# One product by ones instead of eight, for the convolution's mean and mean of squares: VectorE adds the chunks first

## The chip, the cores and the metric

The kernel runs on one core of a Trainium2 chip. The metric is the device time of one execution in microseconds (us): the median of the runs of one kernel. Before the change it is 1557.03 us over three runs (1554.2, 1557.03 and 1557.95).

## What is computed

The program is two transformer blocks one behind the other, on 256 tokens of width 1024, all in float32. Only a piece of the first block matters here, the convolution branch, and in it the layer norm behind the depthwise convolution:

```python
def layer_norm(x, g, b):
    xf = x.astype(jnp.float32)
    mu = jnp.mean(xf, axis=-1, keepdims=True)
    var = jnp.mean(jnp.square(xf - mu), axis=-1, keepdims=True)
    y = (xf - mu) * lax.rsqrt(var + EPS) * g.astype(jnp.float32) + b.astype(jnp.float32)
    return y.astype(x.dtype)

def conformer_conv(u, conv_w, conv_b, ln_g, ln_b, w_pw):
    a, g = jnp.split(u, 2, axis=-1)
    y = a * jax.nn.sigmoid(g)
    y = lax.conv_general_dilated(y, conv_w[:, None, :], ...) + conv_b
    y = jax.nn.silu(layer_norm(y, ln_g, ln_b))
    return y @ w_pw
```

Here `y` has 256 tokens by 1024 channels, and the mean and the mean of squares are taken over the channels. The same block computes queries, keys and values for attention, two gates, and behind them attention, a merge of the branches, and a feed-forward part that gathers single neurons from a table. The second block has two kinds of attention and a mixture of experts.

## The kernel before, in words

The kernel is written out by hand for the five engines: each engine has one instruction stream (`block.tensor`, `block.vector`, `block.scalar`, `block.gpsimd`, `block.sync`), and semaphores join them. Nothing reorders an engine's stream: an instruction that waits holds up all that stands behind it on its engine.

Activations lie with channels on the 128 partitions and tokens along a row, so 1024 channels are K = 8 chunks of 128 x 256. A sum over channels is thus a sum over partitions and chunks. TensorE makes it: `stat` (L643) multiplies by a 128 x 128 matrix of ones and accumulates the chunks in a bank of PSUM, one product a chunk. A float32 product is two MATMUL instructions in the profile, so the eight products of a stat are 16.

The stretch around the change is the projection of the first block, from about 60 to 230 us of the span:

- TensorE follows `first_order()` (L181): pieces `glu` and `gate` of the input projection in split products (L711 and L716), between them the parts of a modulation (`modulation`, L674) and sums of these. Near its end, ahead of the last modulation part (`("part", 7)`), stands `("mean", 0)` (L752): it waits until all eight chunks of the convolution are there (`conv_ready`) and makes the stat "mean". After it come the last modulation part, its sums, and then, once the blocks `w_uq` and `w_ukv` of weights have landed (`use`, L774), eight rounds m = 0 to 7 of the products `q`, `k` and `v` (L776 to L785). After round 1 stands the stat "var" (L787), the mean of squares, which waits for ScalarE's squares (`sq_ready`).
- VectorE makes the depthwise convolution (L1782 to L1799), a chunk m at a time: L1786 gates the chunk, L1789 to L1798 add up 31 taps, L1798 writes chunk m of `convz`. Between chunks it does small jobs for the norms of q and kv (L1800 to L1814). Then it reads the mean (L1818), subtracts it from all chunks (L1820), and takes the `q` tiles out of PSUM as they come, four instructions a round (L1827 to L1832). After round 1 it reads the mean of squares (`inverse("var", D)`, L1752 and L1754), after round 3 it scales the chunks (L1837).
- ScalarE rounds weight pieces for the split products, takes tiles out of PSUM, and squares the centred convolution into `sq` (L1380).
- GpSimd subtracts rounded weights from weights (L1700), one piece of 128 x 1024 after the other, and after the last piece of this stretch spreads a rotated key over the heads in two copies (L1697).
- SyncE loads the weight blocks, all through L543, into a ring of three slots. A load waits until the block three places ahead of it has been used; TensorE tells that with `w_used`, on the first product of the block behind. So the load of `w_ukv` is let go by the first product of the last modulation part, the one behind the stat "mean".

`convz` and `sq` lie in the tile `arena`; `hT`, the normed input of the block, is half of the tile `xh` and is not read any more after GpSimd's first eight subtractions (`h_split`, 63.6 to 69.1 us).

Of the kernel before, what the change touches and what calls it, by code (L numbers as in the profile page):

```python
# [24 lines left out]
ALU = mybir.AluOpType  # L25
# [7 lines left out]
K = D // P  # L33
# [240 lines left out]
def build(nc, w, out):  # L274
# [3 lines left out]
    with ExitStack() as ctx:  # L278
# [29 lines left out]
        hT = xh[:, 1]  # L308
# [174 lines left out]
        gain_ready = sem("gain_ready")  # L483
        ctx_norm_ready = sem("ctx_norm_ready")
        h_ready, h_part, sq_part = sem("h_ready"), sem("h_part"), sem("sq_part")
        in_conv = sem("in_conv")
        qkv_norm_ready = sem("qkv_norm_ready")
        krope_ready, kr_spread = sem("krope_ready"), sem("kr_spread")
# [130 lines left out]
        def _(pe):  # L619
# [124 lines left out]
            for kind, n in first_order():  # L744
                if kind == "part":
                    modulation(4 + n, first_block(2 * n + 1), 1)
                elif kind == "u":
                    pair(TILE[f"u{n}"], use(STREAM["w_in"]), 2 * n, hT, 1 - n)
                elif kind == "mod2_":
                    modulation_sums(TILE[f"mod2_{n}"], 4 + 2 * n)  # L750
                elif kind == "mean":
                    pe.wait_ge(conv_ready, K)  # L752
                    stat("mean", ones, chunks(convz))
                elif kind == "ctx":
                    pe.wait_ge(ctx_norm_ready, 1)
                    pair(TILE["ctx0"], use(STREAM["w_in"]), 2, hcT)
                else:
                    i = FIRST.index((kind, n - n % 2))
                    if i == 0:
                        pair(TILE[f"{kind}{n}"], use(first_block(0)), 2 * n, hT, 1 - n, None if n else (h_ready, 0))  # L760
                    else:
                        ps = tile(TILE[f"{kind}{n}"])
                        for j in range(2):
                            c = 4 * (i - 1) + 2 * (n % 2) + j
                            last = split(ps[:, j * T:(j + 1) * T], c, c + 1, h1_hi, h1_lo, (1 - n % 2) * (1 - j),
                                         None if c else (h_split, 0))
                        last.then_inc(tile_ready, 1)
                if (kind, n) == ("glu", 3):
                    pe.wait_ge(sq_ready, 3)
                    stat("q", ones, chunks(sq[:, 0:2, :]))  # L770
                    pe.wait_ge(sq_ready, 4)
                    stat("kv", ones, [sq[:, 2:4, :].rearrange("p a t -> p (a t)")], 2 * T)
# [3 lines left out]
            for m in range(8):  # L776
                ps = tile(TILE[f"q{m}"])
                group(ps[:, 0:T], proj(uq, 2 * m, cqn, 2048, 2), 1 if m == 0 else 0)
                group(ps[:, T:2 * T], proj(uq, 2 * m + 1, cqn, 2048, 2)).then_inc(tile_ready, 1)

                ps = tile(TILE[f"k{m}"])
                group(ps[:, :], [(ukv[:, m * P:(m + 1) * P], ckvn)]).then_inc(tile_ready, 1)
                ps = tile(TILE[f"v{m}"])
                group(ps[:, :], [(ckvn[:, (m // 2) * P:(m // 2 + 1) * P],
                                  ukv[:, D + (m % 2) * 512:D + (m % 2 + 1) * 512])]).then_inc(tile_ready, 1)  # L785
                if m == 1:
                    pe.wait_ge(sq_ready, 5)  # L787
                    stat("var", ones, chunks(sq))

            pe.wait_ge(kr_spread, 2)  # L790
            for kind, n in order:
# [925 lines left out]
        def _(dve):  # L1717
# [64 lines left out]
            for m in range(K):  # L1782

                dve.wait_ge(tile_free["act"], readers[:TILE[f"glu{m}"] + 1].count("act"))
                y = ypad[:, m % 2, :]
                tt(y[:, HALF:HALF + T], cglu[:, m % 4, 0:T], cglu[:, m % 4, T:2 * T], ALU.mult).then_inc(glu_used, 1)  # L1786
                dve.wait_ge(glu_used, m + 1)
                s = [0, 0]
                s[0] = mark(ts(cacc[:, 0, :], y[:, 0:T], conv_w[:, m * TAPS:m * TAPS + 1], vcol("conv_b", m),  # L1789
                               ALU.mult, ALU.add))  # L1790
                s[1] = mark(ts(cacc[:, 1, :], y[:, 1:1 + T], conv_w[:, m * TAPS + 1:m * TAPS + 2], None, ALU.mult))
                for j in range(2, TAPS):
                    dve.wait_ge(dve_step, s[j % 2])
                    acc = cacc[:, j % 2, :]
                    s[j % 2] = mark(stt(cpart if j == TAPS - 2 else acc, y[:, j:j + T],  # L1795
                                        conv_w[:, m * TAPS + j:m * TAPS + j + 1], acc, ALU.mult, ALU.add))
                dve.wait_ge(dve_step, max(s))
                tt(convz[:, m, :], cacc[:, 0, :], cpart, ALU.add).then_inc(conv_ready, 1)  # L1798
                dve.wait_ge(conv_ready, m + 1)  # L1799
                if m == 2:  # L1800

                    dve.wait_ge(tile_free["act"], readers[:TILE["ctx0"] + 1].count("act"))
                    mark(tt(rt1[64:96, 0, 0:T], krope[64:96, 0:T], rope_tab[64:96, :], ALU.mult))
                    seq(tt(rt1[64:96, 0, T:2 * T], krope[96:128, 0:T], rope_tab[96:128, :], ALU.mult))
                    tt(krope[64:96, 0:T], rt1[64:96, 0, 0:T], rt1[64:96, 0, T:2 * T], ALU.add).then_inc(krope_ready, 1)
                    inverse("q", Q_RANK)
                if m == 3:
                    inverse("kv", KV_RANK, 2 * T)
                if m == 5:
                    r = rstd(3)  # L1810
                    for i in range(2):
                        stt(cqn[:, i, :], cq[:, i, :], vcol("q_g", i), r, ALU.mult, ALU.mult).then_inc(qkv_norm_ready, 1)
                    r = rstd(4, 2 * T)
                    stt(ckvn, ckv, vcol("kv_g"), r, ALU.mult, ALU.mult).then_inc(qkv_norm_ready, 1)  # L1814
# [9 lines left out]
            for m in range(8):  # L1824
                ps = take(TILE[f"q{m}"]).rearrange("p (a t) -> p a t", a=2)
                v1, v2 = (x[64:96, m % 2, :].rearrange("p (a t) -> p a t", a=2) for x in (rt1, rt2))
                nc.vector.tensor_copy(qT[0:64, 2 * m:2 * m + 2, :], ps[0:64])  # L1827
                mark(tt(v1, ps[64:96], tab[64], ALU.mult))
                tt(v2, ps[96:128], tab[96], ALU.mult).then_inc(tile_free["dve"], 1)
                dve.wait_ge(dve_step, step[0])  # L1830
                dve.wait_ge(tile_free["dve"], m + 1)
                tt(qT[64:96, 2 * m:2 * m + 2, :], v1, v2, ALU.add).then_inc(q_ready, 1)  # L1832
                if m == 1:
                    inverse("var", D)
                if m == 3:
                    dve.wait_ge(convc_ready, 1)
                    tt(convz, convz, over(rstd(5), K), ALU.mult).then_inc(convn_ready, 1)  # L1837
# [698 lines left out]
```

## Time and profile before

| | |
|---|---|
| median of three runs | 1557.03 us (1554.2 to 1557.95) |
| the profiled execution's own time | 1562.65 us |
| its span, first to last instruction | 1560.8 us |
| TensorE products, busy | 1305.5 us (84% of the span), 7412 instructions |
| VectorE, busy | 868.6 us (56%), 2078 instructions |
| ScalarE, busy | 536.0 us (34%) |
| GpSimd, busy | 438.4 us (28%) |
| mean granted TensorE clock | 0.874 |
| chain of waits that ended last, by engine | TensorE 56%, DMA 30%, VectorE 8%, ScalarE 4% |

The busy shares are means over stages with different limits; what a change in one stage is worth is read from that stage. The chain of waits follows the work back from the last instruction, at each step to what released it. A timeline lists instructions in order of time: start, length, engine, line, operation, output and inputs with their shapes, and in brackets the idle time ahead of it and what ended that. PE is TensorE, PEld its weight loads, DVE VectorE, ACT ScalarE, POOL GpSimd, SP SyncE. The profiled execution took 5.6 us more than the median of the runs.

### The profile page before, as it was taken

Reading aid. Unit: us, or ns where it says so; the run is one execution under the profiler, and the core shown is the slowest. Engines: PE = TensorE matmul, PEld = TensorE weight load, DVE = VectorE, ACT = ScalarE, POOL = GpSimd, SP = SyncE. Lnnn points to the kernel's source line nnn. Section 1 sums busy time; section 2 is a strip of 40 time slices with the busy share of each in tenths; the row PEclk is TensorE's granted clock in tenths of the full one; section 3 lists DMA queues with packets and bytes.
Section 4 is the critical chain, followed back from the end, with each engine's and each line's share of the span. In section 5 each row is a group of like instructions: output and inputs, shape, how many; then the busy total and the mean of one; then the engine's idle time right before and its main releaser. Section 6 shows DMA issues by size and latency. Waiting matters only on the chain.

```text
span 1560.8 us, 19427 instructions
## 1 busy us (share of the span) xinstructions
PE 1305.5 (84%) x7412; PEld 737.8 (47%) x7412; DVE 868.6 (56%) x2078; ACT 536.0 (34%) x1062; POOL 438.4 (28%) x357
## 2 busy tenths in 40 slices
PE   6999999999798666566667766679999999999997
PEld 4888866697443111111111111118769987454544
DVE  2689685654689889854454444544546533321213
ACT  2244264532334333322322222224685501212112
POOL 0555600061334333333333333310535400000000
PEclk9999999999999676766766666769999999999999
DMA  9466612153999999999999999994223356899994
GB/s 388 169 260 239 235 59 102 48 189 108 401 384 397 422 420 421 421 421 421 421 421 421 422 421 421 422 391 197 108 108 109 109 210 278 322 427 427 428 427 203
DMA packets 53086, 476.00 MB, mean 305 GB/s; under 512 B 6145, under 2 KB 6785, under 8 KB 7553
## 3 DMA queue, kind: packets, MB, share of 16 engines
q0 software_dynamic: 36864, 268.45, 41.6%
q1 hardware_dynamic: 14832, 203.46, 32.5%
q10 hardware_dynamic: 1296, 2.84, 0.5%
q8 instruction: 59, 0.97, 0.2%
q14 instruction: 35, 0.28, 0.0%
HBM read 473.68 MB, written 1.05 MB: 304 GB/s over the span
## 4 chain that ended last, share of the span: by engine, by line
PE 56%; DMA 30%; DVE 8%; ACT 4%; issue 2%; POOL 0%; SPq 0%; DVEq 0%; ACTq 0%
DMA arena<-in_uv,pick 25%; PE psD L638 16%; PE psD L711 7%; PE psD L1142 6%; PE psY L888 6%; PE psD L716 4%; PE psD L845 3%; PE psD L1151 3%; DVE arena L1955 3%; ACT arena L1265 2%; DMA arena<-in_experts 2%; PE psY L819 2%; DMA ring<-in_w_in 2%; PE psY L638 1%; ACT L1265 1%
## 5 line engine op out<-in xcount | busy, mean ns | idle before, releaser
L888 PE MATMUL psY<-arena 64*64 64x512 f32 x2048 | 399.0, 873 | 204.8 <-ACT arena L1265 204.4
L1688 POOL DMA_INDIRECT arena<-in_uv,pick x256 | 239.9, 937 | 432.2 <-PE psY L888 385.3
L888 PEld LDWEIGHTS psY<-arena 64*64 64x64 f32 x2048 | 69.4, 169 | 518.8 <-ACT arena L1265 503.4
L1955 DVE CUSTOM_DVE_ANT_0 arena<-arena,psD 128x1024 f32<-128x1024 f32 x128 | 156.2, 1221 | 162.7 <-DMA arena<-in_uv,pick 162.7
L1265 ACT ACTIVATE arena<-arena,pick 128x64 f32<-128x64 f32 x256 | 88.7, 347 | 387.3 <-DVE pick L1955 358.8
L1265 ACT ACTIVATE arena<-psD 64x512 f32<-64x512 f32 (+4 forms) x128 | 68.2, 538 | 330.0 <-PE psD L1142 105.0
L1955 DVE CUSTOM_DVE_ANT_0 arena<-arena,psY 128x1024 f32<-128x1024 f32 x128 | 153.9, 1214 | 44.2 <-DMA arena<-in_uv,pick 43.5
L1265 ACT ACTIVATE arena<-arena 128x64 f32<-128x64 f32 (+2 forms) x300 | 116.0, 387 | 17.2 <-DVE arena L2312 3.8
L638 PE MATMUL psD<-arena 128*128 128x256 f32 (+4 forms) x352 | 92.2, 404 | 0.7 <-DVE arena L2076 0.7
L1795 DVE SCALAR_TENSOR_TENSOR psY<-arena,pick,psY 128x256 f32<-128x256 f32 x224 | 89.2, 482 | 0.0
L638 PE MATMUL psD<-arena,ring 128*128 128x256 f32 (+1 forms) x304 | 73.9, 401 | 4.1 <-issue 3.6
L1265 ACT ACT_TABLE_LOAD x58 | 74.4, 1283 | 7.2 <-DVE pick L1955 4.5
L638 PEld LDWEIGHTS psD<-arena 128*128 128x128 f32 (+2 forms) x352 | 61.4, 193 | 18.1 <-issue 8.1
L638 PEld LDWEIGHTS psD<-arena,ring 128*128 128x128 f32 x304 | 58.8, 195 | 15.8 <-issue 7.0
L845 PE MATMUL psD<-xh,ring 128*128 128x256 f32 x256 | 63.4, 394 | 2.2 <-DVE xh L1920 1.5
L2384 DVE TENSOR_TENSOR yrow_lo<-psD,yrow_hi 64x512 fp32r<-64x512 f32 x32 | 22.0, 689 | 71.4 <-ACT yrow_hi L1265 70.9
L1700 POOL TENSOR_TENSOR ring_r<-ring,work_r 128x1024 fp32r<-128x1024 f32 x9 | 22.8, 2547 | 133.5 <-ACT work_r L1265 133.5
L845 PEld LDWEIGHTS psD<-xh,ring 128*128 128x128 f32 x256 | 47.2, 194 | 23.7 <-issue 15.2
L1265 ACT ACTIVATE arena<-psY 128x512 f32<-128x512 f32 (+1 forms) x50 | 29.7, 594 | 55.5 <-PE psY L804 35.9
L2377 DVE SCALAR_TENSOR_TENSOR arena<-psD,arena 64x512 f32<-64x512 f32 x16 | 12.1, 756 | 47.8 <-ACT arena L1265 47.6
L1265 ACT ACTIVATE arena<-xh 128x512 f32<-128x512 f32 (+1 forms) x17 | 11.9, 704 | 76.3 <-DVE xh L2249 57.2
L1142 PE MATMUL psD<-arena,xh 128*64 128x512 f32 x160 | 36.5, 594 | 1.1 <-DMA arena<-in_experts 1.1
(373 smaller groups left out, 2316.9 us busy)
## 6 DMA issues: line engine op xcount, KB each, us to landing
arena<-in_experts SPq DMA_DIRECT2D x30, 2048.0 KB, 19.3
ring<-in_w_in SPq DMA_DIRECT2D x18, 2048.0 KB, 9.8
ring<-in_experts SPq DMA_DIRECT2D x18, 2048.0 KB, 17.6
ring<-in_w_mod SPq DMA_DIRECT2D x12, 2048.0 KB, 9.0
ring<-in_w_pq SPq DMA_DIRECT2D x4, 2048.0 KB, 8.3
ring<-in_w_out SPq DMA_DIRECT2D x3, 2048.0 KB, 8.2
ring<-in_w_pw SPq DMA_DIRECT2D x2, 2048.0 KB, 8.0
ring<-in_w_o SPq DMA_DIRECT2D x2, 2048.0 KB, 10.6
```

Source lines behind the costliest of these rows:

```text
L638: last = nc.tensor.matmul(dst, a, b, start=(i == 0), stop=(i == len(pairs) - 1))
L711: last = nc.tensor.matmul(ps, hi[:, k * P:(k + 1) * P], x[:, k, :], start=(k + i == 0), stop=False)
L716: last = nc.tensor.matmul(ps, lo[:, k * P:(k + 1) * P], x_hi[:, k, :], start=False, stop=(k == K - 1))
L819: last = nc.tensor.matmul(aux(m // 2 % 2)[:, (m % 2) * T:(m % 2 + 1) * T], wt[:, k * 512 + (m % 4) * P:k * 512 + (m % 4 + 1) * P], convz[: ...
L845: last = nc.tensor.matmul(ps, wt[:, f * D + k * P:f * D + (k + 1) * P], src[:, k, :], start=(k == 0), stop=(k == K - 1))
L888: last = nc.tensor.matmul(y_of[t][at:at + HALF_P, i * 512:(i + 1) * 512], diag[rows, q % DIAGS, :], seats[q % SEATS][rows, D + c * 512:D + ...
L1142: last = nc.tensor.matmul(psD[bank][lo:lo + 64, :], lhs, wt[:, col:col + 512], start=(k == 0), stop=(k == K - 1))
L1151: last = nc.tensor.matmul(psD[bank][lo:lo + 64, :], hidT[:, f, 64 * side:64 * (side + 1)], wd[:, f * D + 8 * lo:f * D + 8 * lo + 512], sta ...
L1265: return nc.scalar.activation(dst, src, f, **kw)
L1688: nc.gpsimd.indirect_dma_start(seats[q % SEATS], None, w["uv"], bass.IndirectOffsetOnAxis(index[:, q:q + 1], 0)).then_inc(gathered[q % SEA ...
L1795: s[j % 2] = mark(stt(cpart if j == TAPS - 2 else acc, y[:, j:j + T], conv_w[:, m * TAPS + j:m * TAPS + j + 1], acc, ALU.mult, ALU.add))
L1955: nc.vector.tensor_tensor_reduce(u_row, u_row, rows_of[t], 1.0, 0.0, ALU.mult, ALU.add, dots[:, q:q + 1]).then_inc(dot_done, 1)
```

## The change

Both stats keep their places in TensorE's stream, but TensorE now makes one product for each in place of eight. VectorE adds the chunks up ahead of it.

For the mean, VectorE keeps a running sum in chunk 0 of `hT`: after chunk 2 it waits for `h_split` and adds chunks 0 and 1, then chunk 2, and after each of chunks 3 to 7 it adds that one: seven additions of 128 x 256. The last one raises `mean_added`, for which TensorE waits in place of `conv_ready`. Each but the last holds VectorE until it is done (`seq`). For the mean of squares, VectorE halves the eight chunks of `sq` in three additions of 1024, 512 and 256 columns, after the q tile of round 1 and ahead of reading the stat; the last raises `var_added`, for which TensorE waits in place of `sq_ready`.

```diff
@@ block.tensor
                 elif kind == "mean":
-                    pe.wait_ge(conv_ready, K)
-                    stat("mean", ones, chunks(convz))
+                    pe.wait_ge(mean_added, 1)
+                    stat("mean", ones, [hT[:, 0, :]])
...
                 if m == 1:
-                    pe.wait_ge(sq_ready, 5)
-                    stat("var", ones, chunks(sq))
+                    pe.wait_ge(var_added, 1)
+                    stat("var", ones, [sq[:, 0, :]])
@@ block.vector, the loop over the chunks of the convolution
                 if m == 3:
                     inverse("kv", KV_RANK, 2 * T)
+                if m == 2:
+                    dve.wait_ge(h_split, K)
+                    seq(tt(hT[:, 0, :], convz[:, 0, :], convz[:, 1, :], ALU.add))
+                if m >= 2:
+                    add = tt(hT[:, 0, :], hT[:, 0, :], convz[:, m, :], ALU.add)
+                    if m < K - 1:
+                        seq(add)
+                    else:
+                        add.then_inc(mean_added, 1)
                 if m == 5:
@@ block.vector, the loop over the q tiles
                 if m == 1:
+                    dve.wait_ge(sq_ready, 5)
+                    seq(tt(flat(sq[:, 0:4, :]), flat(sq[:, 0:4, :]), flat(sq[:, 4:8, :]), ALU.add))
+                    seq(tt(flat(sq[:, 0:2, :]), flat(sq[:, 0:2, :]), flat(sq[:, 2:4, :]), ALU.add))
+                    tt(sq[:, 0, :], sq[:, 0, :], sq[:, 1, :], ALU.add).then_inc(var_added, 1)
                     inverse("var", D)
```

TensorE's stream at the stat "mean", before. A row is one instruction or a run of equal ones, with the semaphores it waits for; here first the last split product, then the stat, the last modulation part, its sums, and the first product of q:

```order
L716 MATMUL psD<-h_hi,ring_r 128x256 [waits u_lo_ready]
L638 MATMUL psY<-arena,cst 128x256 [waits stat_used,conv_ready]
L638 MATMUL psY<-arena,cst 128x256 x7
L674 MATMUL psY<-ring,cS 2x512 [waits mparts_copied,w_loaded2]
L638 MATMUL psD<-cst,arena 128x2 [waits mparts_copied,tile_free_act]
L638 MATMUL psD<-arena,ring 128x256 [waits qkv_norm_ready,tile_free_act,w_loaded1,w_loaded0]
```

The same place after the change (lines stand one lower down in the file):

```order
L717 MATMUL psD<-h_hi,ring_r 128x256 [waits u_lo_ready]
L639 MATMUL psY<-xh,cst 128x256 [waits stat_used,mean_added]
L675 MATMUL psY<-ring,cS 2x512 [waits mparts_copied,w_loaded2]
L639 MATMUL psD<-cst,arena 128x2 [waits mparts_copied,tile_free_act]
L639 MATMUL psD<-arena,ring 128x256 [waits qkv_norm_ready,tile_free_act,w_loaded1,w_loaded0]
```

Seven products are gone from between the split products and the modulation part, and the stat's wait has changed its name.

VectorE's stream behind the q tile of round 1, after the change (before it, the three additions were not there, and the reading of the stat followed at once on the last instruction of the tile):

```order
L1842 TENSOR_TENSOR arena<-arena 32x512 [waits tile_free_dve,dve_step]
L1845 TENSOR_TENSOR arena<-arena 128x1024 [waits sq_ready]
L1846 TENSOR_TENSOR arena<-arena 128x512 [waits dve_step]
L1847 TENSOR_TENSOR arena<-arena 128x256 [waits dve_step]
L1753 TENSOR_SCALAR work<-psY 128x256 [waits rstd_ready,stat_ready]
L1755 RECIPROCAL work<-work 128x256 [waits stat_used]
L1837 COPY arena<-psD 64x512 [waits tile_ready]
```

The additions stand between the q tile of round 1 and the stat, and the q tile of round 2 stands behind both.

## Rows read from the trace of the kernel before

**Rows 1.** The page's first line.
```profile
span 1560.8 us, 19427 instructions
```
**Rows 2.** The chain of waits, 181 to 206 us: start, us, what.
```profile
181.99 3.46 PE psY L638 x16
185.45 1.83 PE psY L674 x16
...
189.15 2.29 issue
191.44 9.45 PE psD L638 x24
200.90 3.45 PE psY L638 x16
204.35 5.18 PE psD L638 x20
```
**Rows 3.** SyncE's timeline, and the DMA issues with the time to landing.
```profile
186.43 0.33 SPq L543 DMA_DIRECT2D ring<-in_w_ukv  x1
...
ring<-in_w_ukv SPq DMA_DIRECT2D x1, 1024.0 KB, 4.9
```
**Rows 4.** VectorE's timeline, 131 to 205 us.
```profile
131.33 0.42 DVE L1798 TENSOR_TENSOR arena<-psY,arena 128x256 f32<-128x256 f32 x1
131.79 1.92 DVE L1786 TENSOR_TENSOR arena<-arena 128x256 f32<-128x256 f32 x1
...
177.62 0.42 DVE L1798 TENSOR_TENSOR arena<-psY,arena 128x256 f32<-128x256 f32 x1
185.56 0.42 DVE L1818 TENSOR_SCALAR work<-psY 128x256 f32<-128x256 f32 x1 [7.51 <-PE psY L638]
186.01 3.62 DVE L1820 TENSOR_TENSOR arena<-arena,work 128x2048 f32<-128x2048 f32 x1
...
201.43 0.68 DVE L1832 TENSOR_TENSOR arena<-arena 32x512 f32<-32x512 f32 x1
204.39 0.42 DVE L1752 TENSOR_SCALAR work<-psY 128x256 f32<-128x256 f32 x1 [2.27 <-PE psY L638]
```
**Rows 5.** Line L1786 alone, all its instructions: ns minimum, median, maximum.
```profile
L1786 DVE TENSOR_TENSOR arena<-arena x8: 363/1131/2622, 48.9 to 163.4; 128x256 f32<-128x256 f32 x8
```
**Rows 6.** GpSimd's timeline, 131 to 188 us.
```profile
131.05 2.37 POOL L1700 TENSOR_TENSOR ring_r<-ring,hi_a 128x1024 fp32r<-128x1024 f32 x1 [0.64 <-ACT hi_a L1265]
...
177.89 2.40 POOL L1700 TENSOR_TENSOR ring_r<-ring,hi_a 128x1024 fp32r<-128x1024 f32 x1 [3.01 <-ACT hi_a L1265]
180.35 7.14 POOL L1697 COPY arena<-arena 32x4096 f32<-32x4096 f32 x2
```
**Rows 7.** GpSimd's and VectorE's timelines at 328 to 334 us.
```profile
327.81 5.23 POOL L1700 TENSOR_TENSOR ring_r<-ring,work_r 128x1024 fp32r<-128x1024 f32 x2 [2.24 <-ACT work_r L1265]
...
329.30 1.48 DVE L1893 TENSOR_TENSOR arena<-arena 128x512 f32<-128x512 f32 x1
330.70 2.89 DVE L1886 TENSOR_TENSOR merged_lo<-arena,merged_hi 128x512 fp32r<-128x512 f32 x1
```
**Rows 8.** Line L2233 alone: an addition of 1024 columns.
```profile
L2233 DVE TENSOR_TENSOR arena<-arena x1: 1217/1217/1217, 1248.9 to 1248.9; 128x1024 f32<-128x1024 f32 x1
```
**Rows 9.** TensorE's timeline, three products that stand behind idle time.
```profile
403.58 1.13 PE L888 MATMUL psY<-arena 64*64 64x512 f32 x4 [5.83 <-ACT arena L1265]
...
411.83 1.09 PE L888 MATMUL psY<-arena 64*64 64x512 f32 x8 [2.36 <-ACT arena L1265]
...
1329.81 0.55 PE L638 MATMUL psD<-hot,hrow_hi 128*128 128x256 f32 x1 [2.48 <-DVE hot L2332]
```
**Rows 10.** Stretches behind idle time: busy of PE, PEld, DVE, ACT, POOL; clock; DMA.
```profile
191.44:196.44 5.00, 5.00 (x11) 3.52 (x12) 1.19 (x2) 0.14 (x1) 0.00 (x0) 0.53 0.59 174
...
403.58:408.10 4.52, 4.52 (x19) 2.79 (x20) 4.28 (x13) 0.49 (x1) 0.94 (x1) 0.54 1.01 426
411.83:416.00 4.17, 4.17 (x28) 2.15 (x32) 4.00 (x17) 1.81 (x6) 1.87 (x2) 1.00 1.02 424
...
1329.81:1333.10 3.29, 3.29 (x16) 3.29 (x17) 2.84 (x24) 0.60 (x1) 0.00 (x0) 0.55 0.96 408
```

More of the change, by code:

```diff
@@ L485, in build @@
         h_ready, h_part, sq_part = sem("h_ready"), sem("h_part"), sem("sq_part")
+        mean_added, var_added = sem("mean_added"), sem("var_added")
         in_conv = sem("in_conv")
```

## The prediction

> **What bounds the kernel now.** I read the chain of waits first, because it tells which engine a saving has to be taken from. In the stretch of the change it runs through TensorE: the stat "mean" from 181.99 to 185.45 us, the last modulation part and its sums until 189.15, a gap of 2.29 us that the chain can only call "issue", and from 191.44 on the products of q, k and v, with the stat "var" from 200.90 to 204.35 between rounds 1 and 2 [rows 2]. So both stats lie on the path, at 3.46 and 3.45 us. SyncE's timeline and the DMA issues explain the gap: the load of `w_ukv` is issued at 186.43 and takes 4.9 us to land, so it lands at 191.33, and q starts at 191.44 [rows 2, 3]. That load is let go by the first product behind the stat "mean"; what the stat gives back, the load and all behind it get as well.
>
> VectorE's timeline shows what the change has to borrow from. The convolution ends at 178.04 (177.62 + 0.42), and VectorE then waits 7.51 us for the mean [rows 4]. TensorE reaches the stat at 181.99, so chunk 7 was there 3.95 us early. At "var" it is less: VectorE is done with the q tile of round 1 at 202.11 (201.43 + 0.68) and waits only 2.27 us for the stat [rows 4].
>
> **The products removed.** A stat is 16 instructions in 3.46 us, 0.216 each. Two stay, 14 go: 3.03 us less at each stat, if TensorE needn't wait for the sum.
>
> **The sum for the mean.** Seven additions of 128 x 256 with both inputs in SBUF. Alone, such an instruction takes 0.36 us at the least (L1786's minimum) [rows 5], and instructions that wait for the one before follow 0.46 us apart (131.33 to 131.79) [rows 4]; the lower bound is 7 x 0.46 = 3.2 us, or 181.3. The upper bound comes from GpSimd. L1786 has the same shape and a median of 1.131 us [rows 5]: at 131.79 it took 1.92 us and ended at 133.71, 0.29 us after GpSimd's subtraction of 131.05 to 133.42 [rows 4, 6]. An addition with two SBUF inputs thus sits out a GpSimd instruction under way. If each of the seven sat out a whole one, 2.40 + 0.29 us, they would take 18.8 us, to 196.9.
>
> I take a value near the lower end, because an addition mostly stands where L1786 stood and sits out the wait that L1786 would have had. At chunk 4 the addition would end at 133.71 with the GpSimd instruction, and L1786 only 0.46 us later than before, however late the addition came there. So the delay doesn't pile up; between chunks it is 0.5 to 1.4 us. Chunk 7 is then written at about 178.5, and the seventh addition meets GpSimd's subtraction of 177.89 to 180.29 [rows 6]: it ends 0.29 us after it, at 180.6. GpSimd's two copies are queued right behind, from 180.35 on [rows 6]. Who goes first there is shown at 329.30: an addition came in during the first of two GpSimd subtractions queued back to back (327.81, 5.23 us for both) and ended at 330.78, so it went between them; the next addition, issued at 330.70, then had to sit out the second one for 2.89 us [rows 7]. The one that already waits goes ahead of the one queued. By that the sum is ready at 180.6, 1.4 us before TensorE asks for it, and the stat gives its whole 3.03 us: it ends at 182.42, `w_ukv` is issued at 183.40, q starts at 188.41.
>
> The other things that move with it cost nothing. L1820 begins 3 us earlier, meets the first of the two copies in place of the second and ends about 3 us earlier too (3.62 us before [rows 4]); ScalarE's squares follow, well before the q tile of round 1. The copies are pushed back by an addition and by L1820, and are wanted only by the attention scores, behind round 7.
>
> **The sum for the mean of squares.** Here the borrowed time isn't there. All times being 3.03 us earlier, TensorE is done with round 1 at 197.87 (200.90 - 3.03). VectorE is done with its q tile at 199.08 and only then starts to add: 1.22 us for 1024 columns [rows 8], 0.68 for 512 (the length of L1832's 512 columns), 0.42 for 256, and 0.04 between each [rows 4]: 2.44 us, until 201.52. No GpSimd instruction is near by then. TensorE waits from 197.87 to about 201.57, 3.7 us, makes its product in 0.43 and is free at 202.0. Before it was free at 204.35. The change has thus 2.35 us left of its 3.03: at "var" it saves 3.03 on products and pays 3.7 for a wait. VectorE gets the stat at the same moment, and its idle 2.27 us are filled by the additions, so the rounds behind move by the same 2.3 us on both engines.
>
> **The clock.** A wait of 3.7 us has a second price. Behind the idle 2.29 us at 189.15 the granted clock was 0.53 over the next 5.00 us, that is 1.2 GHz nearly throughout; behind 5.83 us at 403.58 it was 0.54 for 4.52 us; behind 2.48 us at 1329.81 it was 0.55 for 3.29 us; behind 2.36 us at 411.83 it stayed 1.00 [rows 2, 9, 10]. Half of the work time at the lower level is lost: 2.4, 2.1 and 1.5 us, a mean of 2.0. So three of four shorter or equal idle stretches were followed by the lower clock, and TensorE is as tight as VectorE in rounds 2 to 7; the loss comes through. I take 2.0: -2.35 + 2.0 = -0.35 us, with bounds of -0.85 and +0.05.
>
> The Trainium skill, page "TensorE: Matmul & The Clock Gate", section "Why this matters for your kernels", warns against idle gaps between bursts of matmuls, since a long one takes the clock to half. By that rule the lower clock behind the new wait would be certain, and the warm case below would have no chance; the 2.36 us of idle time that the clock outlived in this trace [rows 9, 10] are shorter than the new wait, so they don't refute it.
>
> **The sum.** Against the profiled execution (1562.65 us, span 1560.8 [rows 1]) the change gives -0.35. That execution is 5.6 us above the median of 1557.03, more than the whole change is worth; I carry the difference over to the median: 1556.7 us. Behind the stretch every load and gather is started by work on the chain, so the difference should stay what it is until the end.
>
> **Rivals.** (1) *Warm.* The clock holds across the new wait. Then the saving is 2.35 us: 1554.7. For it: the 2.36 us that went unpunished; against it: three others. (2) *GpSimd goes first, once.* The first copy slips in ahead of the seventh addition. A copy is 3.57 us (7.14 / 2), the sum is ready at 180.35 + 3.57 + 0.29 = 184.2, and the stat ends at 184.65, 0.8 us earlier than before and not 3.03. With the clock's 2.0 us and the 0.7 us (3.7 - 3.03) lost at "var": +1.9, 1558.9. Against it: the order at 329.30. (3) *Slower: both copies go first.* The seventh addition ends at 187.49 + 0.29 = 187.8 and the stat at 188.2, 2.8 us later than before; TensorE has then idled 5.8 us there, as long as ahead of 403.58, for which I add 0.5 to 2 us more of low clock on the modulation part; with 0.7 and 2.0 at "var" it makes +6 to +7.5, 1563 to 1564.5. It decides from the point at which the seventh addition ends after 185.0. For it: L1820 did meet these copies before, and took 3.62 us; against it: it would have to lose twice.
>
> **How the numbers follow.** Forecast (cold at "var") 0.68, warm 0.19, one copy first 0.07, both 0.06. The range holds the first three with a spread of the median: the three runs before lie within 2.8 us below and 0.9 above their median. Low: 1554.7 - 1.5 = 1553.2; high: 1558.9 + 0.5 = 1559.4. About 0.3%, 4.7 us, is what a measurement of this kernel can tell from no change. No case comes down to 1552.4; for all I have not seen 0.03. Above 1561.7 lies rival 3 alone: 0.06. The rest, 0.91, is no change that can be told.
>
> **What would show it.** In the profile of the changed kernel the stat "mean" is 2 MATMULs with no idle time ahead of it, the seventh addition ends some 0.3 us behind a GpSimd subtraction, and `w_ukv` is issued about 3 us earlier against the last split product. Ahead of the stat "var" TensorE idles 3 to 4.5 us, released by VectorE's addition, and rounds 2 and 3 run at the lower clock. Wrong would be: idle time at the mean, a full clock behind "var", a reading of the stat later than it was, or a total more than 4.7 us off, which would mean that something outside 178 to 230 us has moved.

## The result, and the profile after

The changed kernel takes 1562.18 us (median of 22 runs) against 1558.68 us of the kernel before (22 runs): a ratio of 1.0022, 95% interval 1.0013 to 1.0030, that is 2.0 to 4.7 us slower. The forecast was 0.35 us faster, its range ended at 1559.4, and neither holds. The profiled execution took 1563.18 us, against 1562.65 before.

First the page of the changed kernel, its first lines [rows 1]:

```profile
span 1561.4 us, 19382 instructions
...
PE 1301.0 (83%) x7384; PEld 731.9 (47%) x7384; DVE 872.3 (56%) x2088; ACT 536.0 (34%) x1062; POOL 440.4 (28%) x357
```

The 28 MATMULs are gone and the ten additions are there. The chain of waits (start, us, what) answers to [rows 2]:

```profile
180.12 0.96 PE psD L717 x8
181.08 0.43 PE psY L639 x2
181.51 1.83 PE psY L675 x16
183.34 1.88 PE psD L639 x16
185.22 2.28 issue
187.50 8.12 PE psD L639 x20
...
197.86 0.68 DVE arena L1842
...
198.57 1.24 DVE arena L1845
...
200.56 0.43 DVE arena L1847
...
201.03 1.22 PE psY L639 x2
```

The stat "mean" lasts 0.43 us and follows on the split products without a gap; from its start to the first product of q it is 6.42 us, 9.45 before. At "var" the chain leaves TensorE for VectorE's additions, as it did not before, and the stat behind them lasts 1.22 us: it runs at the lower clock already (behind the same wait at full clock it takes 0.70 us, as `after_3` shows below).

VectorE's and then GpSimd's timeline of the changed kernel show the seventh addition [rows 4, 6]:

```profile
177.97 0.42 DVE L1799 TENSOR_TENSOR arena<-psY,arena 128x256 f32<-128x256 f32 x1
178.43 1.23 DVE L1814 TENSOR_TENSOR xh<-xh,arena 128x256 f32<-128x256 f32 x1
181.55 0.42 DVE L1828 TENSOR_SCALAR work<-psY 128x256 f32<-128x256 f32 x1 [1.89 <-PE psY L639]
```

```profile
176.98 2.40 POOL L1701 TENSOR_TENSOR ring_r<-ring,hi_a 128x1024 fp32r<-128x1024 f32 x1 [2.79 <-ACT hi_a L1266]
179.45 9.27 POOL L1698 COPY arena<-arena 32x4096 f32<-32x4096 f32 x2
```

It ends at 179.66, 0.28 us behind the subtraction, and the two copies stand behind it: neither of the rivals with GpSimd came. TensorE's windows at the end of the wait for "var" and behind it (the column after the five engines is the granted clock) [rows 10]:

```profile
199.78:201.03 1.25, 0.00 (x0) 0.00 (x0) 1.13 (x3) 0.00 (x0) 0.00 (x0) 0.50 0.00 0
...
201.57:206.58 5.01, 5.01 (x12) 3.63 (x11) 3.04 (x4) 0.00 (x0) 0.00 (x0) 0.50 0.00 0
...
210.00:215.00 5.00, 5.00 (x18) 3.09 (x17) 4.79 (x6) 3.32 (x7) 0.00 (x0) 1.00 0.01 3
```

So the stretch went the way that was forecast, with the lower clock ("cold") behind "var". Its size is another matter. From here on "the stretch" is the time from the start of the stat "mean" to the first product of the run of 12 in the convolution branch (L819 before, L820 after, near 228 us): 46.43 us before and 47.46 after in these two profiles, so 1.03 us longer and not 0.35 shorter. The total is some 3 us longer, so most of the loss lies elsewhere.

### The profile page after: what moved, and what is told of

Same layout as the page of the kernel before. It is cut to its first block, busy times and chain, and to the rows that moved or that the text cites. A ratio compares the mean times of both kernels' runs of the same rounds, so it can differ in the third digit from the quotient of the medians.

```text
span 1561.4 us, 19382 instructions
## 1 busy us (share of the span) xinstructions
PE 1301.0 (83%) x7384; PEld 731.9 (47%) x7384; DVE 872.3 (56%) x2088; ACT 536.0 (34%) x1062; POOL 440.4 (28%) x357
## 4 chain that ended last, share of the span: by engine, by line
PE 51%; DMA 30%; DVE 12%; ACT 4%; issue 2%; POOL 1%; SPq 0%; DVEq 0%; ACTq 0%
DMA arena<-in_uv,pick 25%; PE psD L639 15%; PE psD L712 6%; PE psD L1143 6%; PE psY L889 5%; DVE arena L1969 4%; PE psD L717 3%; PE psD L1152 3%; ACT arena L1266 2%; PE psD L846 2%; DMA ring<-in_w_in 2%; DMA arena<-in_experts 2%; PE psY L820 2%; ACT L1266 1%; PE psY L639 1%
```

## The experiments

Each ratio is to the kernel before, run on the same chip, with its 95% interval in brackets; a gain or loss in us beside it is the ratio's distance from 1 times 1559 us.

**Each half alone.** `mean_only` keeps the stat "var" and its eight products as before, `var_only` the stat "mean".

```diff
mean_only:
-                    pe.wait_ge(var_added, 1)
-                    stat("var", ones, [sq[:, 0, :]])
+                    pe.wait_ge(sq_ready, 5)
+                    stat("var", ones, chunks(sq))
var_only:
-                    pe.wait_ge(mean_added, 1)
-                    stat("mean", ones, [hT[:, 0, :]])
+                    pe.wait_ge(conv_ready, K)
+                    stat("mean", ones, chunks(convz))
```

(VectorE's additions for the other stat go as well.)

> The half for the mean alone: seven additions on VectorE and one product at the stat 'mean', the stat 'var' as before (eight products, no additions). Theory A (the cost of the change sits at the stat 'var': a wait of 3.7 us for VectorE's additions and the low clock behind it): the mean gives its 3.0 us, so 2.5 to 3.5 us faster than the kernel before (ratio near 0.998), no idle time ahead of the stat 'mean', w_ukv let go some 3 us earlier. Rival B (the additions between the chunks of the convolution, or a longer stretch of low clock behind the shorter stat, eat what the mean gives): 0 to 3 us slower than the kernel before.

> The half for the mean of squares alone: three additions on VectorE and one product at the stat 'var', the stat 'mean' as before. Theory A: 3.0 us less of products against a wait of 3.7 us, and 1.5 to 3 us of half clock behind it: 2 to 4 us slower than the kernel before, and with the mean's half this adds up to the changed kernel. Rival B: the wait costs only its own 0.7 us, 0 to 1 us slower.

Measured: `mean_only` 0.9985 (0.9975 to 0.9995), -2.3 us; `var_only` 1.0020 (1.0008 to 1.0033), +3.1 us. TensorE's timelines, of `mean_only` and then of `var_only`:

```profile
179.91 0.60 PE L639 MATMUL psY<-xh,cst 128*128 128x256 f32 x2
...
186.52 4.33 PE L639 MATMUL psD<-arena,ring 128*128 128x256 f32 x10 [2.32 <-issue]
194.99 3.62 PE L639 MATMUL psY<-arena,cst 128*128 128x256 f32 x16
...
222.51 2.75 PE L820 MATMUL psY<-arena,ring 128*128 128x256 f32 x12
```

```profile
180.71 3.62 PE L639 MATMUL psY<-arena,cst 128*128 128x256 f32 x16
...
203.70 1.22 PE L639 MATMUL psY<-arena,cst 128*128 128x256 f32 x2 [3.71 <-DVE arena L1838]
```

The mean's half was priced at -3.03 us, and its interval (-3.9 to -0.8 us) holds that. The other half by the forecast's terms costs 3.7 - 3.03 + 2.0 = 2.7 us, and its interval (1.2 to 5.1 us) holds that too. But the halves sum to +0.8, and both together measured +3.4 (and +2.8 in `after_again`). Some 2 us come only when both are there, though the intervals of the halves leave room for less.

**The clock at "var".** `warm` puts four filler products (products that nobody uses, made by `keep`) ahead of the wait for the sum.

```diff
                 if m == 1:
+                    keep(4, aux(3))
                     pe.wait_ge(var_added, 1)
```

> The whole change, and in the wait ahead of the stat 'var' TensorE makes four products that nobody uses (identity by 512 columns of constants, into a free bank, about 0.86 us each, 3.45 us together). Theory A in its form with the clock: the clock stays at 2.4 GHz behind 'var', so 2 to 3 us faster than the changed kernel for that alone and 0.5 to 2.5 us faster than the kernel before. Rival C (the clock behind 'var' costs nothing on the path, because VectorE is as late): the same time as the changed kernel, 3.5 us slower than before.

Measured: 0.9997 (0.9987 to 1.0007), -0.5 us. TensorE's timeline of `warm`:

```profile
186.93 5.46 PE L639 MATMUL psD<-arena,ring 128*128 128x256 f32 x10 [2.19 <-issue]
200.51 0.70 PE L639 MATMUL psY<-arena,cst 128*128 128x256 f32 x2 [0.28 <-DVE arena L1848]
```

The clock holds behind "var" (0.70 us, not 1.22), and the ratio is 3.9 us below the change's 1.0022, more than the 2.0 priced for the clock. In the profiles, which both had an equally long low clock at q, the stretch of `warm` is 44.69 us, 2.8 less than the changed kernel's 47.46. The wait at q still costs clock: ten products take 5.46 us where 2.75 are enough.

**The place of the sum of squares.** `late_var` moves the stat "var" and its reading one round back, so that TensorE has round 2 to do during the additions; `early_var` moves the three additions ahead of the q tiles.

```diff
late_var, TensorE:
-                if m == 1:
+                if m == 2:
                     pe.wait_ge(var_added, 1)
early_var, VectorE, ahead of the loop over the q tiles:
+            dve.wait_ge(sq_ready, 5)
+            seq(tt(flat(sq[:, 0:4, :]), flat(sq[:, 0:4, :]), flat(sq[:, 4:8, :]), ALU.add))
...
```

> The whole change, but the stat 'var' and VectorE's reading of it stand one round later (behind round 2 of q, k and v), while the additions stay behind the q tile of round 1, so that they lie beside TensorE's round 2. Theory A: no idle time ahead of 'var' and no low clock behind it, both stats give their 3.0 us, less what VectorE adds in its own stream (2.4 us of additions in place of 2.3 us of idle time): 2 to 4 us faster than the kernel before. Rival B: 0 to 3 us slower than before.

> The whole change, but VectorE makes the three additions of squares as soon as ScalarE has them, ahead of the first q tile, where it idles 6.0 us in the changed kernel's trace; the squares were ready at 187.2 us there and the q tile came at 191.3, so the additions (2.4 us) end some 1.5 us before it. Theory A (the cost sits in the wait ahead of 'var' and in the clock behind it): no idle time at 'var', both stats give 3.0 us: 4 to 7 us faster than the kernel before (ratio 0.9955 to 0.9975), and faster than the half for the mean alone. Rival D (a stat of one product costs by itself, whatever it waits for, because TensorE is less busy and the clock falls): no idle time, yet low clock behind 'var', and no faster than the half for the mean alone (-2.3 us).

Measured: `late_var` 0.9993 (0.9980 to 1.0006), -1.1 us, `early_var` 0.9986 (0.9970 to 1.0003), -2.2 us with runs from 1550.9 to 1562.5. In `early_var` the wait is gone:

```profile
177.20 0.60 PE L639 MATMUL psY<-xh,cst 128*128 128x256 f32 x2
...
183.91 4.51 PE L639 MATMUL psD<-arena,ring 128*128 128x256 f32 x10 [2.42 <-issue]
192.57 0.59 PE L639 MATMUL psY<-arena,cst 128*128 128x256 f32 x2
...
217.68 2.75 PE L820 MATMUL psY<-arena,ring 128*128 128x256 f32 x12
```

The stretch is 40.48 us, the shortest so far, yet both versions gave less than was expected (2 to 4 us and 4 to 7 us). The squares were ready well before the q tile of round 1 (at 187.24 us in the changed kernel's trace, where the first q tile came at 191.29); nothing obliged the additions to stand behind it.

**Both kernels again.** `after_again`, `before_again`, `before_3` to `before_5` and `after_3` are unaltered copies, for the scatter of the parts.

> The changed kernel once more, for a second profile. Theory A: again a wait of 3.7 us ahead of 'var', low clock for 3 to 7 us behind it, and the stretch from the stat 'mean' to the first conv product of the attention stage 47 to 48 us long; 2 to 4.7 us slower than before. If the clock stays up behind 'var' in this one, the clock is no fixed part of the cost.

> The kernel before once more, for a second profile. The first one was 4 us above the median of its kernel, and its stretch from the stat 'mean' to the first conv product took 46.4 us with 5.1 us of work at half clock behind the wait for w_ukv. If that low clock is shorter in the usual execution (as in the profile of the mean's half, 3.4 us), the stretch is about 44.8 us here and the change costs 2.7 us in it, near the measured 3.5; if it is the same 46.4, the missing 2.5 us lie outside the stretch.

> The kernel before, a third profile. Two profiles each give 46.4 and 45.8 us for before and 47.5 and 46.4 for the change, from the stat 'mean' to the first conv product: +0.8 us, where the runs say +3. Theory E: in many executions of before the clock does not fall at the wait for w_ukv, or for a shorter time, and the stretch is 43.9 to 45 us; both profiles so far were of executions 4 us above their median. Rival F: the stretch is always near 46, and 2 us are lost elsewhere in the program.

> The kernel before, a fourth profile; as for the third: the stretch takes 43.9 to 45 us by theory E, near 46 us by rival F.

> The kernel before, a fifth profile; as for the third: the stretch takes 43.9 to 45 us by theory E, near 46 us by rival F.

> The changed kernel, a third profile: both theories expect 46.4 to 47.5 us for the stretch, with low clock behind 'var' once more, since the 3.7 us of idle time there are longer than any after which the clock has stayed up in the traces so far.

`after_again` measured 1.0018 (1.0008 to 1.0027): the loss is there again. One execution each of the kernel before took 1562.72, 1556.58, 1554.13 and 1559.88 us. With the padded kernels and those with fillers at the start (below) there are seven profiles of the order before and five of the changed one. Means in us, range in brackets:

| part of the span | order before | changed order |
|---|---|---|
| start to the modulation part at about 52 us | 52.05 (50.49 to 53.66) | 52.68 (50.28 to 53.76) |
| from there to the stat "mean" | 126.97 (126.02 to 128.25) | 127.72 (126.93 to 128.57) |
| the stretch | 46.33 (45.67 to 47.06) | 46.06 (43.81 to 47.46) |
| from there to the end | 1331.8 (1329.0 to 1335.1) | 1332.1 (1329.3 to 1333.6) |

The mean stretch is 0.27 us shorter, near the forecast's 0.35, but that is luck: the two sets don't hold the same amounts of low clock. At q the granted clock was low for 3.4 us in three of the seven profiles before and in four of the five after, and for 6.8 us in the others. Like against like, the stretch is 45.7 us before and 46.3 after (3.4 us at q, cold at "var"), or 46.8 and 47.5 (6.8 us at q, cold at "var"). So with "var" cold the change costs 0.6 to 0.7 us in the stretch, where the forecast had it gain 0.35. `after_3` is the odd one: TensorE's timeline, and the windows behind the wait:

```profile
201.51 0.70 PE L639 MATMUL psY<-arena,cst 128*128 128x256 f32 x2 [3.72 <-DVE arena L1847]
202.04 2.75 PE L639 MATMUL psD<-arena,ring 128*128 128x256 f32 x10
```

```profile
203.00:208.00 5.00, 5.00 (x19) 3.33 (x18) 4.65 (x6) 3.11 (x5) 0.00 (x0) 1.00 0.00 0
```

The same wait of 3.72 us, and the clock stayed at its upper level; the stretch is 43.81 us, 1.9 less than before and 2.5 less than in the cold profiles with the same 3.4 us at q.

**The clock at q.** `before_qwarm` is the kernel before with two filler products ahead of q's wait for its weights.

```diff
+            keep(2, aux(3))
             uq, ukv = use(STREAM["w_uq"]), use(STREAM["w_ukv"])
```

> The kernel before with two useless products (0.86 us each) in the 2.3 us in which TensorE waits for w_ukv. If idle time alone makes the clock fall there, it stays at 2.4 GHz or comes back sooner: 1 to 2.5 us faster than before. If the clock had been lost already in the modulation part and its sums, whose products are small, the low stretch begins at the same place: within 1 us of before.

Measured: 0.9994 (0.9984 to 1.0004). The clock holds, as TensorE's timeline shows:

```profile
189.82 2.82 PE L638 MATMUL psD<-arena,ring 128*128 128x256 f32 x10 [0.38 <-issue]
```

The stretch is 44.02 us, 2.3 less than the mean, but the median gives back only 0.9 us, which is not certain.

**What lies outside: the load of `w_in` at 107 us.** Its time from issue to landing is 12.24 to 12.61 us in the ten profiles that lack one or both halves, and 12.68 to 13.69 us in the ten that have both. The chain of waits has it as a row; here that of the kernel before, `mean_only`, `var_only` and the changed kernel:

```profile
107.11 12.61 DMA ring<-in_w_in
...
128.12 1.21 PE psD L716 x8
```

```profile
107.31 12.32 DMA ring<-in_w_in
```

```profile
106.55 12.44 DMA ring<-in_w_in
```

```profile
107.28 13.46 DMA ring<-in_w_in
...
129.15 1.21 PE psD L717 x8
```

ScalarE's rounding, GpSimd's subtraction and TensorE's products wait for it in a row; the product at 129.15 starts 21.87 us after the issue, 21.01 before (128.12).

What the late landing costs shows when the clock is set aside. Behind that load the granted clock fell for 3.4 us at about 130 us in some executions and not in others; here are the windows of `before`, where it fell, and of `before_3`, where it didn't:

```profile
129.00:136.00 7.00, 7.00 (x49) 7.00 (x49) 6.89 (x14) 2.73 (x5) 4.66 (x3) 0.76 0.44 185
```

```profile
127.00:134.00 7.00, 7.00 (x62) 7.00 (x62) 6.89 (x15) 2.73 (x5) 4.82 (x3) 1.00 0.52 220
```

Without that fall, the part from 52 us to the stat "mean" takes 126.02 to 126.56 us in the six profiles that lack a half, and 126.93 to 127.38 us in the seven with both: 0.9 us more on average, and the ranges don't touch. (With the fall it is 0.4 us more, from four and three profiles, and the ranges do.)

There is a second place of this kind at the end. The last long row of DMA in the chain is a load of experts' weights; here that of the kernel before and of the changed kernel:

```profile
1498.87 30.80 DMA arena<-in_experts
```

```profile
1498.62 31.21 DMA arena<-in_experts
```

From the issue of this load (the third from last of the experts) to the end of the span it is 61.7 to 62.5 us, mean 61.9, in the ten profiles that lack a half, and 62.5 to 63.1 us, mean 62.8, in the ten with both: 0.9 us more, with ranges that just meet. The very last load of the experts lands 32.55 to 33.40 us after its issue in the former and 33.64 to 34.02 in the latter. Between 230 us and there the means differ by 0.4 us, inside a scatter of 5 us.

So the kernels with both halves lose up to 1.8 us at two places far from the change. Add this to the stretch, each version against the kernel before with an equally long low clock at q: +2.4 us for the change cold at "var", -0.3 for `warm`, -1.3 for `late_var`, -3.4 for `early_var`. Measured were +3.4, -0.5, -1.1 and -2.2, and each sum lies within the measured interval. This is a reckoning after the fact, from one profile each of the last three.

Why the loads land later is another question. Up to 178 us `mean_only` and the changed kernel run the same instructions in the same order. What differs there is the length of their programs, and with it perhaps where these lie in memory. `before_pad` and `after_pad` put twenty small memsets at the start of VectorE's program, where it waits 16 us.

```diff
+            for i in range(20):
+                seq(nc.vector.memset(psY[:, 1024 + 4 * i:1028 + 4 * i], 0.0))
             nc.vector.memset(psY[:, 1024:2048], 0.0).then_inc(y_zero, 1)
```

> The kernel before, with twenty memsets of 128x4 on VectorE ahead of its first instruction, where VectorE otherwise waits some 16 us for TensorE: nothing is computed with them and the order of everything else stays. What is looked at lies far ahead of the mean: the load of w_in issued at about 107 us, which landed 12.3 to 12.6 us later in six profiles of kernels that hold no or only one of the two halves of the change, and 13.0 to 13.7 us later in the six that hold both. If the place of the instructions in memory decides that (the fetches of TensorE's program run over the same 16 transfer engines as the weights), the padding alone can move the landing, to 13 us or more, and with it the median by up to about 1 us. If the additions themselves make it late, the landing stays at 12.3 to 12.6 us here and the median within 1 us of the kernel before.

> The changed kernel with the same twenty memsets at the start of VectorE's program. If the place of the instructions in memory decides the landing of w_in, it can move here from the 13.0 to 13.7 us of the kernels with both halves, and the part of the 3 us that lies outside the stretch of the change goes or changes with it: the median then is 1 to 2 us below that of the changed kernel. If the additions themselves cost it, the landing stays at 13.0 us or more and the median stays 2.5 to 3.5 us above the kernel before.

Measured: 0.9999 (0.9987 to 1.0011) and 1.0002 (0.9987 to 1.0017). The chains of `before_pad` and of `after_pad`:

```profile
104.17 12.41 DMA ring<-in_w_in
```

```profile
103.81 13.18 DMA ring<-in_w_in
```

The landings did not move with the padding, against the theory of the place in memory in this form. One rival stayed untested: the twenty profiles split just as sharply by the length of TensorE's program, 7398 to 7418 products in the ten that lack a half and 7384 to 7394 in the ten with both, while VectorE's length doesn't split them (2098 instructions in `before_pad`, 2088 in the changed kernel). Seven filler products in the changed kernel, 14 MATMULs, would have tested it. A fetch of 16 KB of instructions falls into the load's time in every one of the twenty, so its presence is not the difference.

`after_pad`'s excess over the kernel before seemed gone, though its profile has both late loads (33.75 us for the last one); but its interval touches that of the changed kernel: unclear. Its profile has a full clock at 36 us, where the changed kernel's three have 3.4 to 6.8 us at the lower level; hence the next test.

**The clock at 36 us.** `before_swarm` and `after_swarm` are the two kernels with three filler products ahead of the first 64 products of the block.

```diff
             modulation_sums(TILE["mod1_"] + 1, 2)
+            keep(3, psD[3])
```

> The kernel before with three filler products of 512 columns (about 1.45 us) ahead of the first block's first group of 64 products, where TensorE waits 1.32 us for VectorE behind sixteen products of 2 columns. In five profiles of the kernel before, the granted clock is at its lower level for 0 to 6.8 us from 36 us on, and the part of the modulation behind it starts at 50.5, 52.0 or 53.6 us accordingly. If the fillers hold the clock there, that start is 50.3 to 50.8 us and the median 1 to 2 us below the kernel before. If they don't, nothing changes by more than 0.3 us.

> The changed kernel with the same three fillers. If the 3 us by which the changed kernel is slower are made of a longer low clock at 36 us (6.8, 3.4 and 6.8 us in its three profiles), which the change could touch only through the place or the start of its program, the excess over the kernel before with the fillers falls to under 1 us. If they come from behind that (the clock at var, the later landing of w_in, the rest of the kernel), the excess stays 2 to 4 us.

Measured: 0.9999 (0.9987 to 1.0011) and 1.0021 (1.0010 to 1.0033), 1558.63 and 1562.59 us. TensorE's timelines of `before_swarm` and `after_swarm`:

```profile
35.40 4.52 PE L725 MATMUL psD<-cst 128*128 128x512 f32 x6
39.76 13.98 PE L638 MATMUL psD<-xh,ring 128*128 128x256 f32 x64
53.66 1.90 PE L674 MATMUL psY<-ring,cS 128*2 128x512 f32 x16
```

```profile
35.46 4.52 PE L726 MATMUL psD<-cst 128*128 128x512 f32 x6
39.82 13.98 PE L639 MATMUL psD<-xh,ring 128*128 128x256 f32 x64
53.72 1.90 PE L675 MATMUL psY<-ring,cS 128*2 128x512 f32 x16
```

The 64 products run at full clock (13.98 us), but the fillers take the low clock themselves, 4.52 us (three products are six MATMULs, 2.8 us even at full clock, as `early_qswarm` below shows, not the 1.45 I wrote). So they gained nothing; what they do is to make the start equal in both profiles, and the excess is 3.96 us all the same. The clock at 36 us is not its cause: that theory falls, and the likeness of `after_pad` to the kernel before has no cause shown here.

**A version that beats both.** `early_qwarm` joins `early_var` and the fillers at q; `early_qswarm` adds those at the start.

```diff
+            keep(2, aux(3))
             uq, ukv = use(STREAM["w_uq"]), use(STREAM["w_ukv"])
```

> Both halves, with the three additions of squares ahead of the q loop (no wait on TensorE's side at var: early_var measured 0.9986 of the kernel before) and with two filler products ahead of q's wait for its weights (in the kernel before they kept the granted clock at q, 0.9994). If the two gains add up, the stretch from mean to the convolution's first product takes 38.5 to 40.5 us and the median is 3 to 4 us below the kernel before. If the clock at q was not lost in early_var anyway, the fillers only delay q by their own time and the median is that of early_var, about 2 us below the kernel before.

> Early additions of squares, fillers ahead of q, and the three fillers at 36 us: early_qwarm measured 0.996 of the kernel before with no low clock at 36 us in its profile. If its runs mostly escape the low clock there already, the median stays within 0.5 us of it (1552 to 1554 us); if some of them fell into it, it goes down by up to 1 us more and the runs scatter less.

Measured: `early_qwarm` 1552.83 us, 0.9960 (0.9945 to 0.9975), 3.9 to 8.6 us faster than the kernel before; `early_qswarm` 0.9969 (0.9959 to 0.9980). TensorE's timeline of `early_qwarm`, and its clock:

```profile
177.40 0.60 PE L639 MATMUL psY<-xh,cst 128*128 128x256 f32 x2
...
184.00 2.82 PE L639 MATMUL psD<-arena,ring 128*128 128x256 f32 x10 [0.48 <-issue]
...
191.36 0.59 PE L639 MATMUL psY<-arena,cst 128*128 128x256 f32 x2
...
216.94 2.75 PE L821 MATMUL psY<-arena,ring 128*128 128x256 f32 x12
```

```profile
184.00:189.00 5.00, 5.00 (x19) 3.68 (x20) 4.89 (x6) 1.78 (x3) 1.20 (x1) 1.00 0.70 213
191.36:196.36 5.00, 5.00 (x21) 3.65 (x20) 4.79 (x7) 2.88 (x5) 0.00 (x0) 1.00 0.02 10
```

No low clock from the mean to the convolution's products, 39.54 us, 6.8 less than the mean of the kernel before, and the median is 6.2 us down, from five runs. `early_qswarm`, with twelve runs and the same stretch (39.53 us), is 4.8 us down. Both also have the two late loads, so about 5 us were to be expected: here most of the gain of the stretch arrives. The third set of fillers, which in this version ran at full clock (2.82 us), adds nothing.

## Why the prediction was wrong

- **The products removed and the sum for the mean: right.** No idle time at the mean, `w_ukv` issued at 182.49 us, q 3.03 us earlier against the stat. The additions that met GpSimd ended 0.28 us behind it, as the 0.29 of [rows 4, 6] had it. The Trainium skill, page "SBUF — State Buffer", section "SBUF: two separate sides", says that an instruction of VectorE with two SBUF inputs and a GpSimd instruction that reads SBUF shut each other out, whoever starts first going through to its end. The trace agrees (0.28 us), and shows one thing more: the addition that waited went ahead of the copies already queued. (The instruction at 330.70 us in [rows 7], L1886, is a subtraction and not an addition; it has two SBUF inputs all the same.)
- **The sum of squares: right.** The wait was forecast at 3.7 us and is 3.72; the additions take 2.41 us, forecast 2.44.
- **The clock: right in kind, too small in size, and with it the sum for the stretch.** It fell in four of the five profiles of the changed order. There 2.0 us were priced, 2.4 at most. It costs 2.5 us (`after_3` against the three profiles with as long a low clock at q) to 2.8 us (`warm` against the changed kernel): TensorE worked 5.3 to 5.7 us at the lower level there. And of its four idle stretches "shorter or equal" one, 5.83 us, was longer than the new wait. Without the clock the stretch gained 1.9 to 2.1 us, not 2.35. So the term that read -2.35 + 2.0 = -0.35 came out at +0.6 to +0.7. The page "TensorE: Matmul & The Clock Gate" of the Trainium skill, section "Why this matters for your kernels", by which the drop was certain, is contradicted by `after_3` (3.72 us of idle time, the clock at 1.00 behind it): the warm rival had a chance, about one in five here.
- **"Behind the stretch every load and gather is started by work on the chain, so the difference should stay what it is until the end": this step failed, and its silent counterpart ahead of the stretch.** The forecast put everything outside 182 to 230 us at nothing. In the kernels with both halves the load of `w_in` at 107 us, ahead of the change, lands 0.8 us later on average and makes the part up to the stat "mean" 0.9 us longer where the clock doesn't fall; the last loads of the experts' weights land later too, and the end of the span is 0.9 us longer. That makes up to 1.8 us which the forecast lacked. Why the loads land later is open: the halves or the length of TensorE's program go equally well with it. The start up to 53 us is excluded as the cause by `after_swarm`. With 0.6 to 0.7 us in the stretch this is some 2.4 us of the 3.4 measured (2.0 to 4.7); the last 1 us is inside the interval and in no part of the profiles that stands out. The prediction's own sign for such a loss, a total more than 4.7 us off, came: 5.5 us.
- **The carry from the profile to the median and the range: too narrow.** One part of the kernel before, up to 53 us, takes 50.5, 52.0 or 53.6 us in different executions with nothing changed. Three runs of it (1554.2 to 1557.95) had shown less than the 22 (1554.2 to 1562.32), whose median is 1558.7; the changed kernel at 1562.2 would be outside the range even with that.

## What to carry to other kernels

Before a sum is moved to another engine, ask where its inputs are ready, not where its result is read: the same three additions cost a wait and a clock drop behind the q tile and no wait ahead of it. Two filler products (1.96 us) in a wait of 2.3 us held the clock here; three in a wait of 1.3 us gained nothing. A local gain of under a microsecond says nothing of the total when the parts of unaltered kernels scatter by 3 us: compare profiles in which the clock was low at the same places, take each half alone, and let the median of many runs decide.

## What was not expected of the hardware

- The granted clock falls at the same places of a kernel in some executions and not in others: at 36 us for 0, 3.4 or 6.8 us in seven profiles of the order before, and at "var" in four of five with the same idle time.
- The same load lands at different times after its issue in kernels that differ elsewhere: 12.24 to 12.61 us against 12.68 to 13.69 for `w_in`, 32.55 to 33.40 against 33.64 to 34.02 for the last load of the experts. The cause is not shown.
- A stat of two MATMULs behind a wait of 3.7 us took 0.70 us at full clock and 1.22 at half: the granted clock fell during the wait (it was 0.50 from 199.78 us on, 1.25 us ahead of the stat), not after the work began again.
